# Hybrid decoder step on one core: opening order, cache copies, gate units and the last stage's steps rearranged

## The reference, cut to what matters

```python
for i in range(DEPTH):                       # 2 layers: layer A (i = 0), layer B (i = 1)
    hp, hs = rmsnorm(xp, norm_w[i]), rmsnorm(xs, norm_w[i])      # prompt 1024 x 1024, sample 32 x 1024
    mkv = einsum('bmd,de->bme', mem_prompt, w_mem_kv[i])         # 256 memory tokens -> keys and values
    if i % 2 == 0:   # three groups (window, dilation) = (128,1), (512,4), (2048,16), 4 heads each
        yp, bp = layer_a(hp, mk_p, mv_p, w_in_a, w_out_a, rel_bias, None)
        ys, bs = layer_a(hs, cache_mem_k[i], cache_mem_v[i], ..., (cache_win_k0, ..., cache_win_v2))
        # outputs of the sample group: each window cache, moved on by 4 rows: kc[:, L + T - keep:]
    else:            # gated DeltaNet, 8 heads, chunks; conv of width 4; delta state 128 x 128 per head
        yp, cp, dp = layer_b(hp, ..., None, None)
        ys, cs, ds = layer_b(hs, ..., state_conv, state_delta)
    xp, xs = xp + yp, xs + ys                # y = (branch * silu(z)) @ w_out
y_prompt, y_sample = rmsnorm(xp, final_norm_w), rmsnorm(xs, final_norm_w)
```

## Time and profile before

| | |
|---|---|
| median of 3 runs | 2437.03 us (2436.96 to 2442.77) |
| profiled execution, its own time | 2438.38 us |
| its span, first to last instruction | 2436.6 us |
| mean granted TensorE clock | 0.982 of full speed (2.4 GHz) |
| PE / DVE / ACT / POOL busy | 96% / 36% / 29% / 11% |
| moved by DMA | 209.07 MB, 86 GB/s over the span |

### The profile page before, as it was taken

The page is one execution under the profiler, slowest core; times in us unless marked ns, Lnnn a source line. Parts: engine busy times, 40 slices in busy tenths (PEclk is TensorE's granted clock), DMA queues, the critical chain, the costliest instruction groups (busy, mean ns, idle before and its releaser), DMA issues. The chain is left out here.

```text
span 2436.6 us, 45271 instructions
## 1 busy us (share of the span) xinstructions
PE 2339.0 (96%) x19286; PEld 1529.4 (63%) x19286; DVE 873.7 (36%) x2206; ACT 710.7 (29%) x1566; POOL 265.2 (11%) x463
## 2 busy tenths in 40 slices
PE   7999999999999998998898999999998899999998
PEld 5666666666666676553465777777676666664433
DVE  4022232232223224231244555555656323222241
ACT  3011411411241141220242343334334344441101
POOL 0100020020001004000032112212211000020000
PEclk8999999999999998999999999999999999999999
DMA  6622241221211136556246001101010121104441
GB/s 185 227 84 65 66 154 55 61 77 46 70 52 62 35 98 216 176 192 200 79 142 188 20 11 29 29 3 29 21 29 13 43 60 61 44 29 148 133 152 44
DMA packets 205054, 209.07 MB, mean 86 GB/s; under 512 B 14038, under 2 KB 171958, under 8 KB 204063
## 3 DMA queue, kind: packets, MB, share of 16 engines
q1 hardware_dynamic: 192710, 145.91, 20.0%
q0 software_dynamic: 12144, 60.26, 7.1%
HBM read 178.78 MB, written 67.18 MB: 101 GB/s over the span
## 5 line engine op out<-in xcount | busy, mean ns | idle before, releaser
L619 PE MATMUL bank<-arena 128*128 128x352 f32 x2304 | 715.3, 460 | 3.4 <-PEq L248 2.4
L619 PEld LDWEIGHTS bank<-arena 128*128 128x128 f32 x2304 | 424.7, 191 | 210.5 <-issue 5.3
L1607 PE MATMUL bank<-arena 128*128 128x352 f32 x1248 | 453.3, 475 | 0.0
L1607 PEld LDWEIGHTS bank<-arena 128*128 128x128 f32 x1248 | 206.4, 191 | 62.9 <-issue 1.1
L2274 PE MATMUL bank<-arena 128*128 128x352 f32 x672 | 206.4, 462 | 2.0 <-PEq L248 2.0
L1672 PEld LDWEIGHTS bank<-arena 128*32 128x32 f32 x8192 | 137.0, 110 | 109.3 <-issue 32.2
L1672 PE MATMUL bank<-arena 128*32 128x64 f32 x8192 | 169.7, 225 | 18.3 <-issue 9.1
L2723 PE MATMUL bank<-arena 128*128 128x512 f32 x384 | 183.4, 608 | 0.0
L752 ACT ACTIVATE arena<-bank 128x352 f32<-128x352 f32 x144 | 76.6, 532 | 341.1 <-PE bank L619 259.5
L2274 PEld LDWEIGHTS bank<-arena 128*128 128x128 f32 x672 | 125.9, 191 | 66.5 <-issue 3.6
L841 DVE COPY arena<-bank 128x128 f32<-128x128 f32 x96 | 28.0, 292 | 380.4 <-PE bank L691 380.4
(11 more groups left out here) (384 smaller groups left out, 2487.2 us busy)
## 6 DMA issues: line engine op xcount, KB each, us to landing
arena<-in_w_in_a SPq DMA_DIRECT2D x48, 512.0 KB, 3.9
arena<-in_w_in_b SPq DMA_DIRECT2D x40, 512.0 KB, 3.8
arena<-in_cache_win_k SPq DMA_DIRECT2D x48, 256.0 KB
arena<-in_cache_win_v SPq DMA_DIRECT2D x48, 256.0 KB
out<-arena SPq DMA_DIRECT2D x40, 256.0 KB, 3.3
arena<-in_w_mem_kv SPq DMA_DIRECT2D x16, 512.0 KB, 6.2
arena<-in_cache_mem_k SPq DMA_DIRECT2D x32, 256.0 KB
arena<-in_cache_mem_v SPq DMA_DIRECT2D x32, 256.0 KB
```

The source lines that it names most:

```text
L619: m = nc.tensor.matmul(bank[part_][:, 0:PART], ring.slots[:, (B0 + b) % RING, k, :], part_in(k, part_), start=k == 0, stop=k == KD - 1)
L1607: m = nc.tensor.matmul(bank[j % 3][:, 0:PART], ring.slots[:, (B1 + b) % RING, k, :], part_in(k, part_), start=k == 0, stop=k == KD - 1)
```

## The change

Five things are moved; no arithmetic is added or taken away. (1) In the opening SP waits for weight block 0 to have landed before it issues prompt tile 0 and all behind it; DVE evacuates tile XT + 1 before it norms tile 0; in `FRONT` block 5 and table 8 go ahead of tiles 7 and 8. (2) Heads 2 and 3 of layer A issue the copies of the 512-row caches (`ck2`, `cv2`), which layer B's mixer issued before; the 124-row copies (`ck0`, `cv0`), which stood there, go to the start of layer B's memory attention. (3) In layer B's mixer four units leave group 13 (index `NG_ - 3`), four leave the b slots of the last round, and eight stand in its last slot. (4) The last stage begins with four units, and each step's units are four further on. (5) There PE takes two neighbouring steps of kind key or ks together; scores stand behind the units of their own step, not in the next one.

```diff
@@ FRONT
-             ("table", 7), ("tile", 7), ("tile", 8), ("table", 8), ("block", 5), ("block", 6), ("block", 7)]
+             ("table", 7), ("block", 5), ("table", 8), ("tile", 7), ("tile", 8), ("block", 6), ("block", 7)]
@@ opening, SP
             ring.load(sp, 2)
+            sp.wait_ge(ring.loaded[0], 16)
             x_load(0)
@@ opening, DVE
                 if kind == "tile":
-                    if n == XT + 1:
-                        norm(0)
-                    elif n < NT:
+                    if n < NT:
                         norm(n + 1)
...
                     nc.vector.tensor_copy(dest_in(n, 4), bank[2 * (x % 2) + 1][:, 0:4 * r]
                                           .rearrange("p (k r) -> p k r", r=r)).then_inc(ev_v, 1)
+                    if n == XT + 1:
+                        norm(0)
@@ layer A, POOL, head h
-                copy_cache(pool, *((ck1, sk1, 512, DT), (cv1, sv1, 512, DT), (ck0, sk0, 128, DT),
-                                   (cv0, sv0, 128, DT))[h])
+                copy_cache(pool, *((ck1, sk1, 512, DT), (cv1, sv1, 512, DT), (ck2, sk2, 512, 0),
+                                   (cv2, sv2, 512, 0))[h])
@@ layer B, table of units
-    slots = [[(1, 2)] * 4 + [(1, 1)] * 12] * (NG_ - 3) + [[(1, 2)] * 4 + [(0, 0), (0, 0), (0, 1)] * 4]
+    slots = [[(1, 2)] * 4 + [(1, 1)] * 12] * (NG_ - 3) + [[(1, 2)] * 4 + [(0, 0)] * 12]
     slots += [[(0, int(s in RSLOT)) for s in SLOTS]] * 2
-    slots += [[(0 if s not in RSLOT or RSLOT[s][1] == "c" else 1, int(s in RSLOT)) for s in SLOTS]]
+    slots += [[(int(s in RSLOT and RSLOT[s][1] == "a"), int(s in RSLOT)) for s in SLOTS[:15]] + [(0, 8)]]
@@ layer B, POOL
             squares(1)
-            copy_cache(pool, ck2, sk2, 512, 0)
-            copy_cache(pool, cv2, sv2, 512, 0)
@@ memory attention of layer B, POOL
+            copy_cache(pool, ck0, sk0, 128, DT)
+            copy_cache(pool, cv0, sv0, 128, DT)
@@ last stage
-        return range(2 * t - 4, 2 * t - 2) if t >= 2 else ()
-    LAST = NUNIT // 2 + 2
+        return range(2 * t, 2 * t + 2) if t >= 2 else ()
+    FIRST_UNITS = 4
+    LAST = NUNIT // 2
...
                 x.then_inc(ktd, 1)
-                if i:
-                    scores(i - 1)
...
-            for t in range(LAST):
-                if t < len(steps):
-                    kind, i = steps[t]
...
+            for u in range(FIRST_UNITS):
+                unit(u)
+            while t < LAST:
+                paired = t + 1 < LAST and kind_at(t) in ("key", "ks") and kind_at(t + 1) == kind_at(t)
+                both = (t, t + 1) if paired else (t,)
+                for x in both:
+                    if x < len(steps):
+                        sample_step(x)
+                for x in both:
+                    out_units(x)
+                for x in both:
+                    if kind_at(x) == "key":
+                        scores(steps[x][1])
+                t += len(both)
```

More of the change, by code:

```diff
@@ L2495, in units_at @@
     def units_at(t):
-        return range(2 * t - 4, 2 * t - 2) if t >= 2 else ()
-    UNITS0 = NUNIT - 2 * (NUNIT // 2)
-    LAST = NUNIT // 2 + 2
+        return range(2 * t, 2 * t + 2) if t >= 2 else ()
+    FIRST_UNITS = 4
+    LAST = NUNIT // 2
     rows2 = lambda b, o: b[:, o:o + 256].rearrange("p (t i) -> p t i", t=2)
@@ L2631, in state_products @@
                 if not j:
-                    scores(NK - 1)
                     pe.wait_ge(qd, 4)
@@ L2743, in sample_fold, with sample_step, out_units @@
                                      start=True, stop=True).then_inc(yd, 1)
-            for t in range(LAST):
-                if t < len(steps):
-                    kind, i = steps[t]
-                    if kind == "key":
-                        key(i)
-                    elif kind == "val":
-                        value(i)
-                    elif kind == "ks":
-                        state_products(i)
-                    elif kind == "up":
-                        update(i)
-                    elif kind == "probs":
-                        pe.wait_ge(sn, 1)
-                        o = turn_bank(("probs", 0))
-                        for k in range(2):
-                            x = nc.tensor.transpose(o[:, k * P:(k + 1) * P], S_m[:, k, :], ident)
-                        x.then_inc(ktd, 1)
-                    elif kind == "sum":
-                        pe.wait_ge(oc, 1)
-                        nc.tensor.transpose(turn_bank(("sum", 0))[:, 0:P], osum, ident).then_inc(ktd, 1)
-                    else:
-                        delta_step(kind)
+            def sample_step(t):
+                kind, i = steps[t]
+                if kind == "key":
+                    key(i)
+                elif kind == "val":
+                    value(i)
+                elif kind == "ks":
+                    state_products(i)
+                elif kind == "up":
+                    update(i)
+                elif kind == "probs":
+                    pe.wait_ge(sn, 1)
+                    o = turn_bank(("probs", 0))
+                    for k in range(2):
+                        x = nc.tensor.transpose(o[:, k * P:(k + 1) * P], S_m[:, k, :], ident)
+                    x.then_inc(ktd, 1)
+                elif kind == "sum":
+                    pe.wait_ge(oc, 1)
+                    nc.tensor.transpose(turn_bank(("sum", 0))[:, 0:P], osum, ident).then_inc(ktd, 1)
+                else:
+                    delta_step(kind)
+            def out_units(t):
                 for u in units_at(t):
@@ L2772, in _ @@
                     unit(u)
+            for u in range(FIRST_UNITS):
+                unit(u)
+            kind_at = lambda t: steps[t][0] if t < len(steps) else None
+            t = 0
+            while t < LAST:
[10 more added lines that the diff above has]
+                t += len(both)
         @block.scalar
```

## The result

| | before | after |
|---|---|---|
| median of 4 runs | 2436.99 us (2433.47 to 2442.77) | 2412.41 us (2410.44 to 2413.26) |
| profiled execution, span | 2436.6 us | 2411.4 us |
| mean granted TensorE clock | 0.982 | 0.986 |

A forecast was written before the change was run, and what follows sets the result against it. PE, busy 96% of the span, bounds the kernel, so time is won only at its gaps, half clock and changes of work. Opening 10.5, copies 11.1, last stage 4.5 sum to 26.1 us: 2437.0 becomes 2411, range 2404 to 2422.

The forecast's parts named there:

- The opening's start: Opening: block 0 starts at 9.5 us at full clock, table 0 at 25.4 instead of 33.41; 8.0 us won.
- Rival 1: The opening is bound by its input, so most of its gain is lost: 2417.5 us; chance 0.12.
- The opening's end: Opening, blocks 5 and 6 and tile 8: less waiting, block 5 and table 8 at full clock; 2.5 us won.
- The copies: Start of layer B's mixer: without the copies PE's instructions no longer come late; 11.1 us won, 9.1 of it idle time.
- Rival 2: The gaps at the start of layer B's mixer are not the copies': 2422 us; chance 0.10.
- The copies' new places: Copies in layer A's heads 2 and 3 and in the memory attention cost nothing: 0 us each.
- rival 4: The moved copies starve layer A's weights, PE standing most of two copies: 2471 us; chance 0.03.
- The end of the mixer: End of layer B's mixer: PE's wait for POOL stays about 3.8 us, ACT's piece standing before the root; 0 won.
- Rival 3: The wait at the end of layer B's mixer is covered after all, 3.8 us off: 2407 us; chance 0.10.
- The last stage: Last stage: earlier PE start 0.8, paired keys 2.1, paired ks steps 1.6; together 4.5 us won.
- the ks pairs: Last stage: pairing the 16 ks steps saves 0.2 us a pair, 1.6 us in all.
- PE's start: Start of the last stage: PE begins at once instead of waiting for DVE; 0.8 us won.

The follow-up runs named there:

- both orders: Changed kernel with ACT's last root ahead of the last slot's pieces and, in the last stage, SP's state store ahead of the next load: 2399.73 us.
- unpaired: Changed kernel with the last stage's key and ks steps taken one by one: 2419.39 us.
- spread, short runs: Changed kernel with ck2, cv2 copied in layer B's mixer, an eighth at each of groups 0 to 7, in two transfers of 8 KB runs: 2411.82 us.
- copies back: Changed kernel with all four moved copies where they stood before, ck2 and cv2 at the start of layer B's mixer: 2424.41 us.

## Why the prediction was right, point by point

**The opening's start (8.0).** The mechanism holds: DVE's order is the whole of it, 7.9 us. Block 0 at 9.32 (9.5 said), both blocks' end at 16.49 (16.8), table 0 at 25.80 (25.4). What failed is what I did not carry on: that table 0 "waits for `c_samp`" is a gap of 1.94 us, and I priced it only as a start time. Behind it the clock fell, and tile, table and block 3 lost 0.83 + 0.63 + 1.81 = 3.3 us, more than the 2.65 between 10.5 and 7.85. It is not so in every execution. Of the ten profiles with this opening, five show no wait for `c_samp`: there P is 65.0 to 65.6 (65.8 said), since the first two blocks run slower (9.2 to 9.6 us), and the table is there when PE comes. Five show a wait of 0.98 to 1.94. In two of these half clock follows within 3 us (here and with both orders; P 68.40 and 69.45). In two it comes some 27 us later, behind the wait of 1.12 for tile 8, and P is 67.92 and 68.65. In one, with a wait of 1.71, it does not come at all and P is 64.84. So a wait of this size may bring the half clock or not, and what decides it is not shown. Rival 1 did not come: PE waited neither for weights nor for prompt tiles, and the input bound table 0 alone.

**The opening's end (2.5).** 3.5 by the run with DVE's old order, and the shape is as said: block 5 takes 3.74, the wait for tile 8 is 1.13 (1.2 said). But the new order does not keep the half clock away for good: in two profiles ("unpaired" and "spread, short runs") the block behind tile 8, now block 6, takes 5.42 and 6.61 us.

**The copies (11.1).** The size was right: 10.14 in the profiles, 10.8 and 12.0 by putting them back. Rival 2 has fallen, and with it what the Trainium skill, "Runtime: NRT & Kernel Launch", section "Instruction fetch mechanics", would have meant here: crossing a block of code was not hidden while the copies filled the DMA engines, 9.1 us by the gaps. The page's "mostly hidden" does agree with the trace: of the 155 blocks of TensorE's code, 4 were waited for before and none after. That PE's code comes late, which I had only read from a missing releaser, is shown by the transfers of code: each gap begins where a block of 16,384 bytes is used up and ends 1.2 to 1.6 us after the next has landed. The rest of the cause as I put it, "these stand behind the copies' long packets", is not shown. Shorter packets left 5.3 us of gaps, and a late block takes no longer to move than others, it only starts late. The runs show the large gaps only with nearly all engines busy (0.90); with few engines busy at a time there was one of 1.89 us.

**The copies' new places (0, 0).** Right in layer A, and rival 4 has fallen. In the memory attention not quite: the barrier at its end holds PE for 3.72 to 3.74 us in the nine profiles in which POOL issues copies in that stage, and for 3.05 in the four in which it does not. This is the row of "copies back", which answers to the one at 2167.82:

```profile
2177.04 3.67 PE L2721 MATMUL bank<-arena 128*128 128x512 f32 x8 [3.05 <-PEq L248]
```

So the short copies cost 0.7 us there. Why a barrier is longer behind them is not shown.

**The end of the mixer (0).** Right, and for the reason given: the wait is 3.75, as ACT's piece stands before the root. Moving the root confirmed it. Rival 3 has fallen.

**The last stage (4.5).** The profile shows 6.10. Keys gave 0.36 a pair against the singles of before, as said (2.1); the ks pairs gave 0.34 instead of 0.2, so 2.7 instead of 1.6; the waits in the up steps shrank by 0.4, from 5.46 to 5.04. PE's start, 0.8 by my sum, gave 0.14 of idle time (3.72 instead of 3.86), as the barrier itself took 0.7 longer with the copies ahead of it. It lies ahead of the stage's first record, so the 6.10 does not hold it: keys, ks pairs and waits are 2.2, 2.7 and 0.4 of the 6.10. Of the 0.8 left, 0.3 lie behind PE's last record (11.5 us before, 11.2 after); the time at half clock is nearly the same (14.2 and 13.8 us, worth 0.2), and 0.3 stay open.

**The barriers' clock.** No term stood for it. Stretches at half clock after a barrier came out shorter in one place and longer in another (the memory attention's first block 7.73 instead of 6.42), -0.51, -1.77 and +1.17 in three stages for which the forecast was 0. They sum to -1.1 us. With the last stage's 1.6 us over its term they make up most of the 3.6 by which the opening (2.65) and the mixer (0.96) fell short: the mechanisms were as said, but that the total came within 2 us of 2411 is in part luck.

## What to carry to other kernels

Price a wait of PE with the half clock that may follow it: 3.75 us of waiting cost 7, and 1.94 cost 5.2 in the profiled execution, while a wait of 1.71 in another brought no half clock. Where a list of one engine ends in a chain that others wait for, moving work beside the chain helps only if the chain's first instruction does not stand behind that work; the same holds for a queue that issues a load before the store that frees a buffer. A large copy in the background wants neither all engines nor a few for long: with all engines full PE's own code came late (9.1 us), and with two held for 43 us a store and weight blocks did (30 us of waits at PE).

## What the runs showed of the hardware that was not expected

- One HBM copy of two rows of 1 MB ran at 50 GB/s on about two of 16 engines, eight of them at once at 267 GB/s. Spread out in time they cost 41.7 us (2454.1 against 2412.4), issued together 12.0, and in halves with short runs, spread, nothing.
- Blocks 0 and 1 of the opening took 7.17 us in five profiles and 9.2 to 9.6 in seven others with the same instructions, with a granted clock printed as 1.00 in all of them. In the slower ones PE shows 5 and 6 matmul records in the windows 10 to 12 and 12 to 14 us where the others show 11 and 11 ("copies back" and the changed kernel): about half the rate. What sets this is open.
- Of sixteen short-run transfers in a row POOL issued fifteen at once and the last only 50 us later; eight long ones passed at once.
- TensorE's code came in 155 transfers of 16,384 bytes on a queue of their own, and PE stood still at the end of such a block eleven times in four runs while copies were under way.
- A stage in which POOL issued 4 MB of copies ended in a barrier that held PE for 3.72 us, and for 3.05 without them.
